# The second score product of stick-breaking attention contracts over 64 rows instead of 128

## The reference, cut to what matters

```
logits = jnp.einsum('bqhd,bkhd->bhqk', q_blk, kf) * inv_sqrt_d        # contraction over 64
mask = (key_pos[None, :] < q_pos[:, None])[None, None]
log_beta = jax.nn.log_sigmoid(logits)
log_1m_beta = jnp.where(mask, jax.nn.log_sigmoid(-logits), 0.0)
later = lax.cumsum(log_1m_beta, axis=3, reverse=True) - log_1m_beta
wts = jnp.where(mask, jnp.exp(log_beta + later), 0.0)
return jnp.einsum('bhqk,bkhd->bqhd', wts, vf)
```

## Time and profile before

| | |
|---|---|
| median of 3 runs | 1587.28 us (1586.86 to 1590.11) |
| span of the profiled execution, first to last instruction | 1586.6 us |
| PE busy / PEld busy | 1556.0 us (98%) / 1299.3 us (82%) |
| DVE / ACT / POOL busy | 1236.3 us (78%) / 772.7 us (49%) / 1004.9 us (63%) |
| mean granted TensorE clock | 0.997 |
| matmuls | 7926, each with its weight load |
| score products (lines 1542 and 1543) | 320 and 320, from 392.5 to 1239.7 us |

### The profile page before, as it was taken

The page is one execution under the profiler, slowest core; times in us unless marked ns, Lnnn a source line. Parts: engine busy times, 40 slices in busy tenths (PEclk is TensorE's granted clock), DMA queues, the critical chain, the costliest instruction groups (busy, mean ns, idle before and its releaser), DMA issues. The chain is left out here.

```text
span 1586.6 us, 24736 instructions
## 1 busy us (share of the span) xinstructions
PE 1556.0 (98%) x7926; PEld 1299.3 (82%) x7926; DVE 1236.3 (78%) x1658; ACT 772.7 (49%) x1490; POOL 1004.9 (63%) x707
## 2 busy tenths in 40 slices
PE   7999999999999999999998999999999999999998
PEld 6888888888888888888877888888788788888886
DVE  6745424784888889998898988889888756677987
ACT  4422222214666666666665666666666512233342
POOL 4531102431788888888877887889986534456774
PEclk9999999999999999999999999999999999999999
DMA  7633335665434243343595443333422687864552
GB/s 246 231 129 145 133 108 184 241 182 161 128 116 113 79 119 104 108 136 91 174 317 182 121 129 87 111 106 110 119 78 65 206 280 252 262 196 161 184 189 110
DMA packets 164225, 245.79 MB, mean 155 GB/s; under 512 B 47729, under 2 KB 81009, under 8 KB 164098
## 3 DMA queue, kind: packets, MB, share of 16 engines
q1 hardware_dynamic: 164098, 244.20, 49.4%
HBM read 158.15 MB, written 85.99 MB: 154 GB/s over the span
## 5 line engine op out<-in xcount | busy, mean ns | idle before, releaser
L1697 DVE TENSOR_TENSOR_SCAN left<-keep,left 128x512 f32<-128x512 f32 x192 | 301.6, 1571 | 39.9 <-issue 23.4
L1770 POOL TENSOR_TENSOR ring<-raw,ring 128x512 fp32r<-128x512 f32 x138 | 240.1, 1740 | 71.8 <-ACT ring L1600 56.6
L1517 PE MATMUL psum<-hT,ring 128*128 128x512 f32 x644 | 264.1, 410 | 4.9 <-DMA hT<-form_scratch 3.6
L1521 PE MATMUL psum<-hT,ring 128*128 128x512 f32 x644 | 262.5, 408 | 0.0
L1519 PE MATMUL psum<-hT,ring 128*128 128x512 f32 x644 | 261.8, 407 | 0.0
L1606 ACT ACTIVATE keep<-psum 128x512 f32<-128x512 f32 (+3 forms) x320 | 170.9, 534 | 139.8 <-PE psum L1543 131.6
L1613 ACT ACTIVATE wt<-psum 128x512 fp32r<-128x512 f32 (+3 forms) x320 | 170.8, 534 | 104.8 <-PE psum L1551 102.0
L1703 DVE TENSOR_TENSOR wt<-psum,wt 128x512 fp32r<-128x512 f32 (+3 forms) x320 | 189.6, 593 | 11.6 <-ACT wt L1613 8.5
L1563 PEld LDWEIGHTS psum<-wt,vm 128*128 128x128 f32 x1088 | 170.9, 188 | 26.6 <-issue 1.5
L1563 PE MATMUL psum<-wt,vm 128*128 128x256 f32 x1088 | 181.3, 281 | 0.4 <-DVE row_sum L1712 0.4
L1551 PE MATMUL psum<-ident,left 128*128 128x128 f32 x1088 | 170.9, 272 | 2.5 <-DVE wt L1703 2.3
(11 more groups left out here) (232 smaller groups left out, 3338.7 us busy)
## 6 DMA issues: line engine op xcount, KB each, us to landing
raw<-in_w_strips SPq DMA_DIRECT2D x92, 256.0 KB, 4.0
qm<-qk_scratch SPq DMA_DIRECT2D x128, 128.0 KB, 4.1
gate<-gate_scratch SPq DMA_DIRECT2D x64, 256.0 KB, 4.5
hT<-form_scratch SPq DMA_DIRECT2D x28, 512.0 KB, 8.6
xt<-in_x SPq DMA_DIRECT2D x16, 512.0 KB, 5.0
xT<-in_x_T SPq DMA_DIRECT2D x16, 512.0 KB, 3.9
qk_scratch<-staging SPq DMA_DIRECT2D x32, 256.0 KB, 2.8
qk_scratch<-store_lo SPq DMA_DIRECT2D x32, 256.0 KB, 3.5
```

The source lines that it names most:

```text
L1517: pe.matmul(o, hi, m_hi, start=k == 0, stop=False)
L1521: last = pe.matmul(o, lo, m_hi, start=False, stop=k == HK - 1)
L1697: dve.tensor_tensor_scan(left[:, n % LN, span][:, ::-1], k, k, carry, ALU.mult, ALU.bypass).then_inc(scanned, 1)
L1770: pool.tensor_tensor(out_, a, b, op).then_inc(s, 1)
```

## The change

The second matmul of `score` takes rows 0 to 63 of both operands, where it took all 128. In the result the product of the low query parts with the low key parts falls away, as it does in `split3`. The first matmul, the loads of `qm` and `km` (rows 64 to 127 of the low queries are still loaded, and not read), the waits, the semaphores and the order of the instructions on every engine stay as they are. PE has 6067 rows in its program before and after. In the built program the second matmul's tile size is 64 x 128 at position (0, 0), and that of every other matmul 128 x 128; its weight load is narrowed in the same way. Lines behind 1543 move down by one.

```diff
                 keys = km[:, t % KN, 0:w]
                 pe.matmul(bank_s(n)[:, 0:w], qm[:, u % QN, 0, cols], keys, start=True, stop=False)
-                pe.matmul(bank_s(n)[:, 0:w], qm[:, u % QN, 1, cols], keys, start=False, stop=True).then_inc(scored, 1)
+                pe.matmul(bank_s(n)[:, 0:w], qm[0:HD, u % QN, 1, cols], km[0:HD, t % KN, 0:w], start=False,
+                          stop=True).then_inc(scored, 1)
```

## The result

The changed kernel takes 1692.97 us (median of 3 runs, 1692.26 to 1696.45) against 1587.28 us: ratio 1.0661, 95% interval 1.0634 to 1.0688. It is slower by 105.7 us, as forecast in sign and inside the range of 1585 to 1725, and 36 us above the point of 1657.

A forecast was written before the change was run, and what follows sets the result against it. PE was taken to bound stage 3, so added PE time counts in full: 1586.6 us plus 640 passages at 0.11 us (70 us) gives 1657 us. The range for 8 in 10 was 1585 to 1725 us.

The forecast's parts named there:

- What bounds the kernel: Stage 3, 400 to 1200 us: PE, busy 788.7 of 800 us, sets the time; DVE at 90% is next.
- One for one: Stage 3: whatever PE takes longer reaches the end in full; only 11.3 of 800 us are idle on PE.
- 640 passages: Score products: PE goes from 128 rows to 64 and back in each of 320 items, 2 passages each.
- The price of a passage: Each change between 128 and 64 rows: exposed weight load of 0.11 us, 640 times, 70 us in all.
- What takes some of it up: PE's idle time in stage 3: largest pieces 7.2 us, waits for loads; none counted on to hide the price.
- The next bound up, 109 us: Load goes ahead, but the product waits for the one before to end: 0.17 us a passage, 109 us.
- B, full serialization: Each passage: load behind the product's end, product behind the load, both ways; 170 us more, 1757 us; chance 0.15.
- A, a free passage: Changing between 128 and 64 rows costs nothing, as with the change to fp32 transposes; 1587 us; chance 0.36.
- C, faster: Items with 256 or 128 keys: loading 64 rows takes half the time, saving 3.5 us; 1583.1 us; chance 0.05.
- The signs in the profile: Wide items: line 1543's load about 0.2 us later, step 0.34 us instead of 0.24, likewise at filler; DVE about 83%.

## Why the prediction was right, and where it was off

**What bounds the kernel: right.** The whole rise lies between the first and the last score product, PE shows no idle time there any more, and DVE, ACT and POOL got slack. The other stages kept their length, and the clock stayed at 1.00. "One for one" holds only after PE's own waits, 17.5 us, have been used up.

**640 passages, each with a price, and nothing for the product itself: right.** That this was the form of the cost was a choice in the prediction, not in the rows of before. Now it is shown from four sides: more 64-row products with the same passages (1.0693), fewer than 128 rows without a passage (1.0017), half the passages with the same products (1.0329), and the same arithmetic without any (1.0002).

**The price of a passage: the term that was mis-sized.** The prediction took 0.11 us, the exposed load alone, and had it start when the stream has passed. The load is exposed, but starts 0.09 us later than that, so a passage costs 0.19 to 0.20 us in the wide items, and all 640 cost 122.9 us where the sum had 70. The choice of 0.11 wasn't drawn from a row with two tile sizes; the sign came right because any price at all is a rise, and the range held because it reached from a free passage to 0.22 us.

**What takes some of it up: put at nothing, and 17.4 us.** The prediction said that nothing hides the price and counted on none of PE's idle time. The passages took up nearly all of it: 11.3 us by the windows, 17.4 by the steps. The two errors partly cancel: 52.9 us too little for the passages, 17.4 too much for what takes them up.

**The next bound up, 109 us,** had the load ahead and the product waiting until the one before had ended. It comes near the measured 104.6 by luck: the rows show the load itself held back, its 0.17 us for a passage is too small, and it too leaves out the 17.4 us that are taken up.

**B, full serialization, 0.27 us:** right in its form (the load behind the product ahead, the product behind the load, both ways) and too large in its number. It let the load begin at the end of the product as the trace models it, 0.39 us after its start, and it begins after 0.31: the drawn duration is longer than what holds the load back. Its reason, the common bank, isn't needed: the filler behind the second product writes to another bank and waits as long.

**A, a free passage,** was argued from the fp32 transposes, which follow `float32r` products without a gap. That remains true in the changed kernel and says nothing about tile sizes: the two are different kinds of change. The rule of the Trainium skill (TensorEngine Tiling (Array Packing), section Key Properties) that a change of tiling mode drains the TensorE is borne out here: the load is held back for 0.31 us behind 512 columns. The Trainium skill also says that a load's time doesn't go by its rows (TensorE: Matmul & The Clock Gate, section LDWEIGHTS (loading the stationary operand)); that holds too, with 183 ns against 189. It didn't help, since the cost isn't in the load's length but in its start.

**C, faster:** its condition, a load that shortens with its rows, doesn't hold (183 ns against 189), and the passage wasn't free.

**The signs in the profile:** the late load came, 0.31 us after the product ahead and not 0.2, and the step grew to 0.42 and 0.43 us and not 0.34, in both directions. DVE fell to 80% of the stretch from 400 to 1200 us where 83% was forecast, in keeping with the larger price:

```profile
400.00:1200.00 800.00, 800.00 (x4010) 601.94 (x4011) 640.78 (x764) 467.91 (x917) 569.52 (x425) 1.00 0.40 115
```

## What to carry to other kernels

Before narrowing the contraction of a matmul in a stream that keeps TensorE full, look whether the instruction still gets the tile size of its neighbours: 96 rows kept it here and were free, 64 and 32 didn't and cost about 0.2 us at each change, in and out. Where a product needs few rows, fill the others with zeros or with a term that does no harm, or put all products of one tile size next to each other, so that the price is paid once for the group. And read such a price from the start of the weight load: that it no longer goes ahead is seen at once in the timeline, while the busy shares only say that PE is at 99%.

## What the runs showed of the hardware

- A weight load of another tile size than the product in flight is held until about 0.09 us after that product's columns have had their time at the usual pace: 0.32 us from its start with 512 columns (median of 224), 0.15 us with 128 (median of 32). Between equal sizes it starts together with that product (0.05 us after it behind the second product of a 128-key item).
- The price is the same into 64 rows and out of them, behind a score product and behind a `weigh` (the kernel with both products over 64 rows), and the same for 32 rows (1.0665) as for 64 (1.0661).
- The profile draws a product whose load is late as beginning with the load, 0.11 us too long (0.50 for 0.39 us). Idle time of PE in it is less than what PE loses by waits: 11.3 against 17.5 us in stage 3 of the kernel before.
